# Gated DeltaNet block on Trainium2: key norms as row factors of the solve, no w product, last output tile in two passes

## The reference, cut to what matters

```python
xn = rms_norm(h, norm1); proj = xn @ w_in
q, k, v = split(silu(causal_depthwise_conv(qkv, conv_qkv)))   # 4 taps
q = l2_normalize(q); k = l2_normalize(k)                      # x / sqrt(sum x^2 + eps), per head
# chunks of 64 positions, gc = cumsum of the log decays g:
a_mat = strict(k_beta @ k.T * decay); k_beta = k * beta; v_beta = v * beta
u_val, w_cum = solve(a_mat + I, [v_beta, k_beta * exp(gc)])
v_new = u_i - w_i @ state;  o_i = q_dec @ state + (q @ k.T * decay) @ v_new
state = state * g_last + k_dec.T @ v_new
o = rms_norm(o, o_norm) * silu(z)
mixed = sigmoid(gate_a) * (o @ w_dn_out) + sigmoid(gate_b) * (short gated conv @ w_sc_out)
h = h + mixed @ w_o
h = h + (silu(gt) * up) @ w_down                              # gt, up from rms_norm(h, norm2) @ w_gate_up
return rms_norm(h, final_norm)[:, N_META:]
```

## Time and profile before

| what | value |
|---|---|
| median of the runs | 1100.43 us |
| the profiled execution's own time | 1099.78 us |
| its span, first to last instruction | 1097.8 us |
| mean granted TensorE clock | 0.997 |
| TensorE (PE) busy | 1077.6 us, 98% |
| ScalarE (ACT) busy | 467.8 us, 43% |
| GpSimd (POOL) busy | 551.3 us, 50% |
| VectorE (DVE) busy | 339.0 us, 31% |

### The profile page before, as it was taken

The page is one execution under the profiler, slowest core; times in us unless marked ns, Lnnn a source line. Parts: engine busy times, 40 slices in busy tenths (PEclk is TensorE's granted clock), DMA queues, the critical chain, the costliest instruction groups (busy, mean ns, idle before and its releaser), DMA issues.

```text
span 1097.8 us, 20326 instructions
## 1 busy us (share of the span) xinstructions
PE 1077.6 (98%) x8301; PEld 915.6 (83%) x8301; DVE 339.0 (31%) x595; ACT 467.8 (43%) x1027; POOL 551.3 (50%) x479
## 2 busy tenths in 40 slices
PE   6999999999999999999999999999999999999996
PEld 6999999999999898978788888878888888888884
DVE  6344545454554545351100112222111111200002
ACT  5565656564746564743422233443222233322221
POOL 4363545444453545363544555655555555555551
PEclk9999999999999999999999999999999999999998
DMA  4222212222212122122522322222232223232322
GB/s 180 75 83 69 78 59 70 78 68 76 72 60 87 60 68 79 59 66 71 173 95 80 112 78 96 96 96 96 96 96 87 92 91 96 97 96 96 96 77 77
DMA packets 27788, 95.45 MB, mean 87 GB/s; under 512 B 2984, under 2 KB 3240, under 8 KB 27696
## 3 DMA queue, kind: packets, MB, share of 16 engines
q1 hardware_dynamic: 26496, 91.77, 25.3%
q10 hardware_dynamic: 1200, 2.38, 0.6%
HBM read 92.03 MB, written 2.11 MB: 86 GB/s over the span
## 4 chain that ended last, share of the span: by engine, by line
PE 95%; DVE 2%; issue 1%; POOL 1%; ACT 0%; DMA 0%; DVEq 0%; SPq 0%; POOLq 0%
PE bank L910 94%; DVE qkv L668 0%; DVE h L905 0%; PE bank L981 0%; POOL w_lo L292 0%; DMA h_in<-h_t 0%; DVE qkv L660 0%; DVE cv L668 0%; PE bank L1098 0%; DVE x_lo L672 0%; POOL x_lo L298 0%; PE bank L977 0%; PE bank L976 0%; ACT cbuf L397 0%; DVE h L902 0%
## 5 line engine op out<-in xcount | busy, mean ns | idle before, releaser
L292 POOL TENSOR_TENSOR w_lo<-w_raw,w_hi 128x512 fp32r<-128x512 f32 x324 | 426.1, 1333 | 489.4 <-ACT w_hi L373 489.3
L910 PE MATMUL bank<-x_hi,w_hi 128*128 128x258 f32 (+2 forms) x896 | 248.2, 335 | 5.5 <-DVE x_lo L672 4.5
L373 ACT ACTIVATE w_hi<-w_raw 128x512 fp32r<-128x512 f32 x324 | 190.1, 623 | 107.1 <-PE bank L910 106.7
L910 PE MATMUL bank<-x_hi,w_lo 128*128 128x258 f32 (+2 forms) x896 | 230.6, 316 | 0.0
L910 PE MATMUL bank<-x_lo,w_hi 128*128 128x258 f32 (+2 forms) x896 | 230.1, 315 | 0.0
L910 PE MATMUL bank<-og_hi,w_hi 128*128 128x512 f32 x416 | 164.7, 396 | 0.0
L910 PEld LDWEIGHTS bank<-x_hi,w_hi 128*128 128x128 f32 x896 | 147.0, 189 | 21.0 <-issue 4.3
L910 PE MATMUL bank<-og_hi,w_lo 128*128 128x512 f32 x416 | 164.3, 395 | 0.0
L910 PE MATMUL bank<-og_lo,w_hi 128*128 128x512 f32 x416 | 164.3, 395 | 0.0
L910 PEld LDWEIGHTS bank<-x_hi,w_lo 128*128 128x128 f32 x896 | 147.0, 188 | 11.2
L910 PEld LDWEIGHTS bank<-x_lo,w_hi 128*128 128x128 f32 x896 | 147.5, 189 | 8.6
(11 more groups left out here) (240 smaller groups left out, 1276.6 us busy)
## 6 DMA issues: line engine op xcount, KB each, us to landing
w_raw<-w_stream SPq DMA_DIRECT2D x162, 512.0 KB, 3.3
h_in<-h_t SPq DMA_DIRECT2D x4, 528.0 KB, 5.0
h<-h_t ACTq DMA_DIRECT2D x1, 2048.0 KB, 9.8
out<-h SPq DMA_DIRECT2D x8, 256.0 KB, 2.1
h_in<-gc_dram SPq DMA_DIRECT2D x7, 264.0 KB, 3.2
cst<-consts SPq DMA_DIRECT2D x1, 512.0 KB, 8.0
h_in<-gc_dram ACTq DMA_DIRECT2D x1, 264.0 KB, 3.0
sm<-small SPq DMA_DIRECT2D x1, 80.5 KB, 6.1
```

The lines of the kernel that those rows point to most:

```text
L292: nc.gpsimd.tensor_tensor(w_lo[:, n % 2, at], w_raw[:, n % 3, at], w_hi[:, n % 2, at].bitcast(f32), ALU.subtract).then_inc(wlo_ready, 1)
L373: return nc.scalar.activation(to, x, ACT.Copy)
L910: return nc.tensor.matmul(o, w, x, start=start, stop=stop)
```

## The change

- Keys are no longer normalised. At step 21 TensorE turns the raw keys of the next head; ScalarE squares the turned tiles with `accum_out`, which gives the sum of each row (a token), and makes rn = 1/norm and rn2 = 1/norm^2 on 128x4 numbers. They enter as factors of rows: beta rn2 in am, beta rn in vb, and -beta exp(gc) rn2 (kse) in the new step below. kdec is copied at step 23. The two TensorE sums over channels and the multiplication of the keys are gone. The same for the meta tokens, on 16x1 numbers, at step 27 of ScalarE and step 0 of VectorE.
- w is not formed. Per chunk there are now three steps in place of two: ks = k^T state and q state (14, 17, 20, 23), r = vb + kse ks on VectorE and vn = um r (15, 18, 21, 24), state and output (16, 19, 22, 25).
- Moved: turned meta tiles and meta k k^T from step 0 to 25, k turned from step 0 to 21, k q^T from step 1 to 5, the output's norm by some five steps, into the next head's steps 1 (sums, root), 3 (VectorE), 4 and 5 (og_hi, og_lo), with six trailing steps behind the last head. The preload of the table set with Ln and Exp goes from quarter 2 to quarter 0 of block c.
- The last tile of w_down runs twice over its 22 k tiles, 256 tokens each time; the last weight block is kept in og_hi and og_lo for the second pass. Tiles 0 to 6 are multiplied by the final norm's gain earlier (ScalarE, in the w_down blocks). Behind each pass: add, square, sums, Ln, Exp, all 256 wide; then VectorE multiplies tiles 0 to 2, 3 to 4 and 7, GpSimd tiles 5 to 6, and four stores follow.

The diff, cut (12 leading spaces of each line taken off):

```diff
...
+            if step == 1 and h >= 1:
+                act.wait_ge(o_sums, h)
+                inverse_root(flat(osq), dbank[0][:, :], 1.0, 1).then_inc(o_root, 1)
+            if step == 4 and h >= 1:
+                act.wait_ge(ogf_ready, h)
+                copy(og_hi[:, h - 1, :], flat(xd)).then_inc(oghi_ready, 1)
...
-            if step == 1:
-                act.wait_ge(k_turned, h + 1)
-                for to, factor, first in ((kbe, be, 0), (kdec, erev, 1)):
-                    for j in range(NJ):
-                        ins = nc.scalar.activation(to[:, j, :], dbank[0][:, 128 * j:128 * (j + 1)], ACT.Copy,
-                                                   scale=factor[:, first + j, h:h + 1])
-                ins.then_inc(kd_ready, 1)
...
-            if step == 15:
-                act.wait_ge(w_done, h + 1)
-                nc.scalar.activation(flat(nwt), dbank[0][:, :], ACT.Copy, scale=-1.0).then_inc(nwt_ready, 1)
...
+            if step == 27 and nxt < HEADS:
+                act.wait_ge(mpre_done, nxt + 1)
+                link(nc.scalar.activation(mvnew, dbank[2][0:META, 0:128], ACT.Square,
+                                          accum_out=ss[0:META, 0:1]))
+                link(nc.scalar.activation(ss[0:META, 0:1], ss[0:META, 0:1], ACT.Ln, bias=eps[0:META, 0:1]))
+                nc.scalar.activation(rn[0:META, 0:1], ss[0:META, 0:1], ACT.Exp, scale=-0.5)
+                nc.scalar.activation(rn2[0:META, 0:1], ss[0:META, 0:1], ACT.Exp, scale=-1.0).then_inc(km_root, 1)
             if nxt < HEADS:
-                if step == 20:
-                    act.wait_ge(qkv_ready, 3 * nxt + 2)
-                    nc.scalar.activation(sqm[:, :], qkv[:, 1, 0:META], ACT.Square).then_inc(km_squared, 1)
                 if step == 21:
-                    act.wait_ge(qkv_ready, 3 * nxt + 2)
-                    link(nc.scalar.activation(flat(am), qkv[:, 1, META:L], ACT.Square))
-                    copy(flat(k_hi), flat(am)).then_inc(k_squared, 1)
-                if step == 24:
-                    act.wait_ge(k_sums, nxt + 1)
-                    act.wait_ge(km_copied, nxt + 1)
-                    inverse_root(sqm[:, :], sqm[:, :], 1.0, 0)
-                    inverse_root(flat(am), dbank[2][:, :], 1.0, 0).then_inc(k_root, 1)
-                if step == 24 and h >= 0:
-                    act.wait_ge(o_added, h + 1)
-                    copy(flat(qo_hi), flat(osq)).then_inc(o_high, 1)
+                    act.wait_ge(k_turned, nxt + 1)
+                    for j in range(NJ):
+                        nc.scalar.activation(am[:, j, :], dbank[0][:, 128 * j:128 * (j + 1)], ACT.Square,
+                                             accum_out=ss[:, 1 + j:2 + j]).then_inc(act_chain, 1)
+                    chain[0] += NJ
+                    act.wait_ge(act_chain, chain[0])
+                    link(nc.scalar.activation(ss[:, 1:], ss[:, 1:], ACT.Ln, bias=eps[:, 0:1]))
+                    nc.scalar.activation(rn[:, 1:], ss[:, 1:], ACT.Exp, scale=-0.5)
+                    nc.scalar.activation(rn2[:, 1:], ss[:, 1:], ACT.Exp, scale=-1.0).then_inc(k_root, 1)
+                if step == 23:
+                    if h >= 0:
+                        act.wait_ge(ds_done, (NJ - 1) * (h + 1))
+                    for j in range(NJ):
+                        ins = nc.scalar.activation(kdec[:, j, :], dbank[0][:, 128 * j:128 * (j + 1)], ACT.Copy,
+                                                   scale=erev[:, 1 + j, nxt:nxt + 1])
+                    ins.then_inc(kd_ready, 1)
...
+        act.wait_ge(h2_squared, m + 1)
+        nc.scalar.activation(h1[:, m, :], h1[:, m, :], ACT.Copy,
+                             scale=sm[:, NORMF + m:NORMF + m + 1]).then_inc(h2_scaled, 1)
+act.wait_ge(sqf_ready, KT - 2)
+for i, half in enumerate(th):
+    act.wait_ge(half_ready, i + 1)
+    nc.scalar.activation(sqt[:, (KT - 1) % 2, half], h1[:, KT - 1, half], ACT.Square).then_inc(half_squared, 1)
+    act.wait_ge(last_sums, i + 1)
+    link(nc.scalar.activation(tg[:, half], dbank[i][:, 0:T // 2], ACT.Ln, scale=1.0 / D, bias=eps[:, 0:1]))
+    nc.scalar.activation(last_rs[i], tg[:, half], ACT.Exp, scale=-0.5).then_inc(half_root, 1)
+    nc.scalar.activation(rs2[:, half], tg[:, half], ACT.Exp, scale=-0.5).then_inc(half_root_sb, 1)
...
+                dve.wait_ge(km_root, h + 1)
+                mult(bv[0:META, 0:1], beta[0:META, 0, h:h + 1], rn[0:META, 0:1])
+                mult(bk[0:META, 0:1], beta[0:META, 0, h:h + 1], rn2[0:META, 0:1]).then_inc(km_scaled, 1)
+                dve.wait_ge(km_scaled, h + 1)
...
+            if 14 <= step <= 23 and step % 3 == 2 and h >= 0:
+                j = (step - 14) // 3
+                dve.wait_ge(vb_ready, h + 1)
+                dve.wait_ge(ks_done, NJ * h + j + 1)
+                nc.vector.scalar_tensor_tensor(vb[:, j, :], dbank[1][:, 128:256], kse[:, h % 2, j:j + 1],
+                                               vb[:, j, :], ALU.mult, ALU.add).then_inc(r_ready, 1)
...
             if step == 0:
-                pe.wait_ge(k_ready, h + 1)
                 pe.wait_ge(egc_ready, h + 1)
                 for j in range(NJ):
                     ins = mm(dbank[1][:, c128[j]], kh[:, tok[j]], kh[:, tok[j]])
                 ins.then_inc(kk_done, 1)
-                if h:
-                    pe.wait_ge(o_root, h)
-                turn(dbank[2][:, 0:128], kh[:, 0:128], ident)
-                turn(dbank[2][:, 128:256], vh[:, 0:128], ident)
-                mm(dbank[2][0:META, 256:272], kh[:, 0:META], kh[:, 0:META]).then_inc(mpre_done, 1)
                 pe.wait_ge(vb_ready, h + 1)
+            if step == 1 and h:
+                pe.wait_ge(o_split, h)
+                spread_sums(dbank[0], flat(qo_hi), flat(o_lo)).then_inc(o_sums, 1)
+            if step == 5:
+                pe.wait_ge(qkv_ready, 3 * h + 1)
+                pe.wait_ge(mu_ready, h + 1)
                 for j in range(NJ):
-                    ins = turn(dbank[0][:, c128[j]], kh[:, tok[j]], ident)
-                ins.then_inc(k_turned, 1)
-            if step == 1:
-                pe.wait_ge(qkv_ready, 3 * h + 1)
-                if h:
-                    pe.wait_ge(ogf_ready, h)
-                for j in range(NJ):
-                    ins = mm(dbank[3][:, c128[j]], kh[:, tok[j]], qh[:, tok[j]])
+                    ins = mm(dbank[0][:, c128[j]], kh[:, tok[j]], qh[:, tok[j]])
                 ins.then_inc(qk_done, 1)
...
-            if step == 15:
-                pe.wait_ge(u_updated, len(LEVELS) * (h + 1))
-                for j in range(NJ):
-                    ins = mm(dbank[0][:, c128[j]], kbe[:, j, :], um[:, j, :])
-                ins.then_inc(w_done, 1)
-            if 16 <= step <= 22 and step % 2 == 0 and h >= 0:
-                j = (step - 16) // 2
+            if 14 <= step <= 23 and step % 3 == 2 and h >= 0:
+                j = (step - 14) // 3
                 if j == 0:
-                    pe.wait_ge(nwt_ready, h + 1)
+                    pe.wait_ge(kd_ready, h + 1)
                     pe.wait_ge(qdec_ready, h + 1)
-                if j == NJ - 1 and nxt < HEADS:
-                    pe.wait_ge(km_copied, nxt + 1)
                 pe.wait_ge(state_ready, NJ * h + j + 1)
-                mm(dbank[1][:, 0:128], um[:, j, :], vb[:, j, :], stop=False)
-                mm(dbank[1][:, 0:128], nwt[:, j, :], state[:, :], start=False).then_inc(vn_done, 1)
+                mm(dbank[1][:, 128:256], kh[:, tok[j]], state[:, :]).then_inc(ks_done, 1)
                 mm(dbank[3][:, c128[j]], state[:, :], qdec[:, j, :], stop=False)
-            if 17 <= step <= 23 and step % 2 and h >= 0:
-                j = (step - 17) // 2
+            if 15 <= step <= 24 and step % 3 == 0 and h >= 0:
+                j = (step - 15) // 3
+                if j == 0:
+                    pe.wait_ge(u_updated, len(LEVELS) * (h + 1))
+                pe.wait_ge(r_ready, NJ * h + j + 1)
+                mm(dbank[1][:, 0:128], um[:, j, :], vb[:, j, :]).then_inc(vn_done, 1)
+            if 16 <= step <= 25 and step % 3 == 1 and h >= 0:
+                j = (step - 16) // 3
...
+                kx = k_raw[nxt % 2]
                 if step == 21:
+                    pe.wait_ge(qkv_ready, 3 * nxt + 2)
                     if h >= 0:
-                        pe.wait_ge(vn_ready, NJ * (h + 1) - 1)
-                    else:
-                        pe.wait_ge(tokens_ready, 1)
-                    pe.wait_ge(km_squared, nxt + 1)
-                    mm(dbank[1][:, 256:256 + META], ones, sqm[:, :]).then_inc(km_sums, 1)
-                if step == 23:
-                    pe.wait_ge(km_copied, nxt + 1)
-                    pe.wait_ge(k_split, nxt + 1)
+                        pe.wait_ge(qkt_ready, h + 1)
+                    for j in range(NJ):
+                        ins = turn(dbank[0][:, c128[j]], kx[:, tok[j]], ident)
+                    ins.then_inc(k_turned, 1)
+                if step == 25:
+                    pe.wait_ge(qkv_ready, 3 * nxt + 3)
```

(74 more changed lines are left out.)

236 lines of the change are left out of this document (123 added, 113 removed).

## The result

The changed kernel takes 1102.60 us (median of 17 runs, 1100.92 to 1103.78), the kernel before 1099.75 (17 runs, 1099.45 to 1100.97): ratio 1.0023, 95% interval 1.0015 to 1.0030. It is slower by 2.85 us, 0.26%. Forecast were 1099.7 and "no change" as likeliest; the range, 1092 to 1105, holds the result, the sign was given 0.22. The profiled execution of the changed kernel took 1102.56 us, its span is 1100.8 against 1097.8.

A forecast was written before the change was run, and what follows sets the result against it. TensorE, busy 98% of the span, was taken to bound the kernel. Terms -12.7 + 7.0 + 5.5 + 2.4 - 2.9 = -0.7 against 1099.78 us gave 1099.1, as median 1099.7; range 1092 to 1105.

The forecast's parts named there:

- What leaves TensorE: In each head, the k sums, meta sum and w's four products leave TensorE: 1.58 us a head, -12.7 us.
- Wait 1: Block b: TensorE waits for um before the first level, 0.8 us in 7 heads, 1.3 in the first: +7.0 us.
- at least 0.25 us left: Slack claimed for second-half weights, levels 2 to 4 and output scaling, which hang on VectorE's same row in block b.
- Wait 2: Before block u: TensorE waits for w_lo, 0.6 us in 7 heads, some 1.3 ahead of head 0: +5.5 us.
- The rival of slow squares: ScalarE's step 21: squares with accumulation are slow; at 0.22 us per square +5.4 us, 1105. Chance 0.22.
- Wait 3: Last head, gb3 to sc3: table loads wait for the sums; 9.45 us, TensorE waits 3.4 for 0.94: +2.4 us.
- 1.3 us a switch: ScalarE's cost per table switch, taken from the trace; the skill's added drain would make the forecast 2.8 us higher.
- The end: Last w_down tile in two passes, only 1 MB left to store behind the last: end at 1094.9, -2.9 us.
- The sum: All terms together: -0.7 us against the profiled execution of 1099.78 us, so 1099.1; 1099.7 as median of the runs.
- The waits are small: Rival on TensorE's waits in the heads: at their low bounds or less, 1088 to 1096, centre 1093. Chance 0.28.
- 0.14 us per square: Threshold for slow squares: from this much beyond 0.05 us, the kernel is slower by over 0.2%.
- A wait inside steps 14 to 25: Sign that would show the forecast wrong: TensorE waiting in these steps of a head, where it saw none.

The follow-up runs named there:

- the fastest version: Changed kernel with mu, um, w_lo, block u's and sc3's weights ahead, one table load, and block u evacuated ahead of step 0: 1087.30 us, ratio 0.9884.

## Why the prediction was wrong

- **What leaves TensorE, -12.7.** Right. The kernel before with less work gave 7.1 of 7.2 us. The rest was not left out by itself; but a head of the fastest version, less its 0.46 us at mt, takes 56.02 us, and 57.53 - 1.58 = 55.95 was the sum without waits. With mu, um and w_lo ahead the first level starts 5.63 us after k k^T without a wait (410.41 to 416.04), the number forecast.
- **Wait 1, +7.0.** Right in size: 0.76 us in 7 heads and 1.2 in the first, 6.5. Its reading was too narrow: what makes it is not um's place but the length of VectorE's row, and putting um ahead gained nothing.
- **The step that failed** is the sentence behind wait 1, that the second-half weights, levels 2 to 4 and the output's scaling have "at least 0.25 us left". The scaling had less than nothing: k q^T came 0.5 to 0.6 us late in 7 heads, and the kernel was 4.3 us faster when that link alone was cut. I had moved xd into the row and og_hi ahead of mu, but had looked only for who reads xd, not for what is queued behind og_hi on ScalarE, which waits for it. That is the move's own rule: an added wait is paid by everything behind the waiting instruction. The row was also longer than like rows: xd's product with zs took 0.99 us for 0.69, the second cv 1.32 for 0.84 in the kernel before.
- **Wait 2, +5.5.** The mechanism was right, the size too large: 0.36 x 7 and 1.14 ahead of head 0, 3.7; removing it gave 3.5. The squares with accumulation were cheaper than I took them:
```profile
400.78 0.28 ACT L546 ACTIVATE am<-bank 128x128 f32<-128x128 f32 x1 [0.16 <-PE bank L1147]
400.96 0.20 ACT L546 ACTIVATION_READ_ACCUMULATOR am<-bank 128x1 f32 x1
401.05 0.27 ACT L546 ACTIVATE am<-bank 128x128 f32<-128x128 f32 x1
...
401.96 0.30 ACT L550 ACTIVATE h_in<-h_in,eps 128x4 f32<-128x4 f32 x1
```
From the first square to w_hi, which started at 402.50, it is 1.72 us, and 1.93 in my sum (1.14 + 0.2 + 0.35 + 0.24). The rival of slow squares, the main weight of "slower", is refuted.
- **Wait 3, +2.4.** Right, 9.43 us for 9.45, and so was the choice of 1.3 us a switch: the Ln starts 1.29 us after its load (528.22 to 529.51), the Exp 1.30. What I left out is what follows a wait of 3.2 us: 1.54 us of slow products.
- **The end, -2.9.** Right: -2.95 between the profiles, -3.1 alone on the kernel before. The first store of the second half stood 4.9 us ahead of the end:
```profile
1092.32 0.42 DVE L959 TENSOR_TENSOR h<-bank,h 128x256 f32<-128x256 f32 x1 [2.80 <-PE bank L973]
...
1095.88 0.97 SPq L287 DMA_DIRECT2D out<-h  x2
```
- **The sum.** From -0.7 to the +3.0 of the profiles are 3.7 us: +4.3 (mu), +1.5 (clock), -1.8 (wait 2), -0.5 (wait 1) and -0.3 (gate blocks) make 3.2. The last 0.5 us lie in the heads. The 0.07 us a head by which 56.02 is over 55.95 would be as much in 8 heads; that the moved work costs this more is not shown. That the result lies inside the range is in part luck: two terms that were at nothing, +5.8 us, and two that were too large, -2.3 us, stood against each other.
- **The rivals.** "The waits are small" did not come: the waits were there, and the 1087.3 us need other orders than those of the change. The rival for "slower" named the squares; of the two causes that made it slower, the late mu and the slow products, it has neither. Its threshold is also misworded: by its own prices 0.14 us per square in all, 0.09 beyond the 0.05, reaches 1102.6. "A wait inside steps 14 to 25" did not occur, nor did one for r.

## What to carry to other kernels

When work leaves the engine that bounds, walk through every other engine's queue in the new order and ask of each instruction that waits what stands behind it, not only who reads its result; a 0.16 us copy behind such a wait cost 4.3 us. If several waits start from one instruction and run through one engine's row, to reorder within the row hands the wait on; only shorter work, another engine or idle time ahead of the row helps, and the consumer at the row's end can be cut loose. A single wait can also slow the products behind it, so a long one deserves its own line in the sum.
